# Opening of a two-block transformer kernel on one Trainium2 core: another order of loads and features, and products of zeros on TensorE

## The chip, the core and the metric

The kernel runs on one core of a Trainium2 chip, in one launch. The metric is the device time in microseconds (us) from the start of the program to its end. In the views of the profile PE is TensorE (PEld its weight loads), DVE is VectorE, ACT is ScalarE, POOL is GpSimd and SP is SyncE, which here only issues transfers (DMA).

## What is computed

Two transformer blocks over 256 tokens of width 1024, all in fp32. The first block has two layers with adaptive normalization and 256 context tokens beside the 256 tokens of x. The change touches only the first lines of layer 0:

```python
shift, scale, gate = adaln(c, ada_w[i], ada_b[i])          # silu(c) @ ada_w + ada_b
cshift, cscale, cgate = adaln(c_ctx, ada_w[i], ada_b[i])
h = rms_norm(x, pre_g[i]) * (1.0 + scale) + shift
hc = rms_norm(xc, pre_g[i]) * (1.0 + cscale) + cshift      # xc is the context
...
p = t @ w_in                                               # t is h, then hc; w_in is 1024 x 4096
q, k, v, z = jnp.split(p, ...)
```

After it come differential attention, a projection, a second layer with grouped attention, and a second block with sparse attention, retention and a gated feed-forward network. None of that is changed.

## The kernel before

**Products.** A product of features and weights in fp32 is made from three products in the rounded format fp32r: each operand is split into a rounded part (`hi`) and its rest (`lo`), and TensorE adds hi·hi, hi·lo and lo·hi in one PSUM bank (lines 746, 747, 748, in this order: `x_hi`·`w_hi`, `x_hi`·`w_lo`, `x_lo`·`w_hi`). Each moves 512 columns. A unit `gemm_unit(stage, c, t, ks)` does this for token tile t (0 and 1 are x, 2 and 3 the context), weight chunk c (512 columns) and the feature blocks `ks` of 128; `FIRST` is blocks 0 to 3, `SECOND` blocks 4 to 7. The projection of the first layer is the stage `in0`, with 8 chunks.

**Modulation.** `ada_half("ada0", c, h)` multiplies the silu of c and c_ctx (`cstat`) by half h of chunk c of `ada_w` (L768, fp32, 4 calls that appear in the trace as 8 records). Chunk 0 is the shift and chunk 2 the scale of feature blocks 0 to 3, chunks 1 and 3 those of blocks 4 to 7; `ADA0_ORDER` is 0, 2, 1, 3. ScalarE copies the rows out (`move`, L1297), `mod_columns` turns them into columns on TensorE (L782), and VectorE adds bias and gain (`mod_sums`, L1900 and L1905).

**Features.** ScalarE sums the squares of each token tile (`norm0_square`, L1254), GpSimd takes the power -1/2, VectorE scales the tile (`norm_in`, L1808, into `zbuf`, here called `xn`), and TensorE transposes it by blocks (`norm0_part`, L865, for blocks 0 to 3; `norm`, L813, for the others). Then `norm_modulated` on ScalarE and `norm_lo_modulated` on VectorE make, from the bank of each block, the modulated features of x (ScalarE, L1268) and of the context (VectorE, L1816) in `sc`, their rounded part `act_hi` (ScalarE, L1274) and the rest `act_lo` (VectorE, L1820), always 512 tokens at a time. TensorE waits for `act_ready` of block k before the first product with it.

**Loads.** SyncE issues the large loads from one queue, in the order of its program: c, c_ctx, the identity, then halves of 1 MB (1024 KB) each. ScalarE's queue loads x (1 MB) and small vectors; GpSimd's the rotary tables and other parameters. `modulation(c)` loads the two halves of chunk c of `ada_w` into four large buffers that are free at this time (`act_hi_as_f`, `kT`, `act_lo_as_f`, `vbuf` for chunks 0, 1, 2, 3). `stream(n)` loads half n of all later weights into one of six buffers (`raw`); from n = 6 on it waits until TensorE has emptied the buffer. A half is split by ScalarE (L1234) and VectorE (L1768) into `w_hi` (a ring of 3) and `w_lo`.

**Order.** Each engine has its own program, written out by hand; nothing is scheduled by a planner. On TensorE the opening is: the transposed silu; both halves of chunk 0 (`ada0(0)`); the transposed parameter vectors (L873); the columns of chunk 0; the transposes of x and then of the context; chunk 2 and its columns; chunk 1; and then the first units of `in0` with blocks 0 to 3, between which lie the transposes of blocks 4 to 7, the columns of chunk 1, and chunk 3 with its columns:

```python
ada0(2)
mod_columns(0, 2)
ada0(1)
gemm_unit("in0", 0, 0, ks=FIRST)
norm("norm0", range(4, 6))
mod_columns(0, 1)
gemm_unit("in0", 0, 1, ks=FIRST)
ada0(3)
gemm_unit("in0", 0, 2, ks=FIRST)
mod_columns(0, 3)
gemm_unit("in0", 0, 3, ks=FIRST)
norm("norm0", range(6, KT))
```

Then the same four units go through blocks 4 to 7, and `in0` goes on chunk by chunk.

## Time and profile before

| | us |
|---|---|
| median of 3 runs | 856.02 |
| lowest and highest | 856.01, 857.07 |
| the profiled execution | 854.07 |
| its span | 852.1 |
| PE busy in the span | 804.9 |
| DVE, ACT busy | 495.9, 395.1 |

The span is the time from the first to the last instruction of the profiled execution; 1.97 us of that execution lie outside it. All rows are from this execution. A row of the timeline gives the start, the duration, the engine, the line, the operation, and the count of instructions that it merges; in brackets stands how long the engine was idle before it, and what ended that. The end of a matmul is modelled and overlaps the next one, so two neighbouring rows are compared by their starts.

### The profile page before, as it was taken

How to read it: one execution, taken by the hardware profiler on the slowest of the kernel's cores; microseconds unless marked ns; L12 is line 12 of the kernel's file. 1: busy time of each engine (PE TensorE's matmuls, PEld its weight loads, DVE VectorE, ACT ScalarE, POOL GpSimd, SP SyncE). 2: the span in 40 equal slices, each digit the busy share in tenths (PEclk: the TensorE clock that was granted, in tenths of full speed). 3: DMA queues.
4: the chain of work that ended last, by engine and by line, in shares of the span. 5: the costliest groups of instructions: out<-in, count | busy, mean ns of one | idle time of the engine just before them, and what ended most of it. 6: DMA issues, size and time to landing. Idle time of an engine off the chain costs nothing. (4 is left out here: it accounts for less than half of the span.)

```text
span 852.1 us, 10720 instructions
## 1 busy us (share of the span) xinstructions
PE 804.9 (94%) x4000; PEld 621.2 (73%) x4000; DVE 495.9 (58%) x849; ACT 395.1 (46%) x718; POOL 39.9 (5%) x55
## 2 busy tenths in 40 slices
PE   4999999999998998999999999998989999999997
PEld 2577788776665677777766787776768888888886
DVE  3373433225557665779655666598786655545553
ACT  4342232326766672575655454544244443344431
POOL 1020000000001000011000001100010000000000
PEclk9999999999999999999999999899989999999999
DMA  9963554325000043239223034863114466646521
GB/s 344 386 207 117 198 197 178 107 111 198 2 1 0 1 150 123 100 101 346 93 78 99 1 128 172 295 231 100 38 49 142 162 221 204 198 149 210 186 98 50
DMA packets 70438, 122.92 MB, mean 144 GB/s; under 512 B 2618, under 2 KB 28556, under 8 KB 70260
## 3 DMA queue, kind: packets, MB, share of 16 engines
q1 hardware_dynamic: 69344, 119.85, 40.7%
q0 software_dynamic: 512, 1.18, 0.5%
q10 hardware_dynamic: 532, 1.21, 0.4%
q8 instruction: 32, 0.52, 0.3%
q14 instruction: 18, 0.15, 0.1%
HBM read 121.17 MB, written 1.06 MB: 143 GB/s over the span
## 5 line engine op out<-in xcount | busy, mean ns | idle before, releaser
L746 PE MATMUL psum<-w_hi,act_hi 128*128 128x512 f32 (+1 forms) x720 | 293.5, 408 | 2.1 <-DVE act_lo L1820 0.8
L747 PE MATMUL psum<-w_lo,act_hi 128*128 128x512 f32 (+1 forms) x752 | 293.5, 390 | 0.0
L748 PE MATMUL psum<-w_hi,act_lo 128*128 128x512 f32 (+1 forms) x720 | 281.0, 390 | 0.0
L1768 DVE TENSOR_TENSOR w_lo<-raw,w_hi 128x2048 fp32r<-128x2048 f32 (+1 forms) x79 | 178.7, 2266 | 147.3 <-ACT w_hi L1234 147.1
L1234 ACT ACTIVATE w_hi<-raw 128x2048 fp32r<-128x2048 f32 (+1 forms) x79 | 149.6, 1895 | 121.0 <-PE psum L748 46.3
L746 PEld LDWEIGHTS psum<-w_hi,act_hi 128*128 128x128 f32 x720 | 136.3, 189 | 56.8 <-issue 26.5
L747 PEld LDWEIGHTS psum<-w_lo,act_hi 128*128 128x128 f32 x752 | 142.5, 190 | 26.3 <-issue 1.2
L748 PEld LDWEIGHTS psum<-w_hi,act_lo 128*128 128x128 f32 x720 | 136.1, 189 | 29.3
L1736 POOL TENSOR_TENSOR rstd<-ms,half_neg 128x1 f32<-128x1 f32 (+3 forms) x38 | 33.5, 883 | 593.5 <-DVE ms L1791 593.5
L1368 ACT ACTIVATE sc<-psum,nmax 128x512 f32<-128x512 f32 (+1 forms) x64 | 36.7, 581 | 30.5 <-DVE nmax L1959 30.5
L1959 DVE TENSOR_REDUCE nmax<-psum 128x2 f32<-128x1024 f32 (+1 forms) x32 | 30.5, 956 | 33.1 <-PE psum L897 33.0
L846 PE MATMUL psum<-ident,sc 128*128 128x128 f32 x192 | 31.9, 282 | 18.2 <-DVE sc L1974 10.1
L846 PEld LDWEIGHTS psum<-ident,sc 128*128 128x128 f32 x192 | 21.6, 142 | 23.8 <-DVE sc L1974 13.7
L1297 ACT ACTIVATE sc<-psum 128x512 f32<-128x512 f32 (+1 forms) x60 | 32.3, 538 | 8.9 <-PE psum L846 8.0
L1297 ACT ACTIVATE qT<-psum 128x512 f32<-128x512 f32 (+1 forms) x24 | 13.2, 569 | 49.7 <-PE psum L840 32.9
L1198 PE MATMUL psum<-w_hi,act_hi 128*128 128x512 f32 x88 | 34.3, 390 | 0.8 <-DVE act_lo L2513 0.8
L1200 PE MATMUL psum<-w_hi,act_lo 128*128 128x512 f32 x88 | 34.3, 389 | 0.0
L1199 PE MATMUL psum<-w_lo,act_hi 128*128 128x512 f32 x88 | 34.2, 389 | 0.0
L1692 ACT ACTIVATE sc<-psum 128x256 f32<-128x256 f32 x22 | 8.4, 383 | 47.2 <-PE psum L748 47.2
L897 PE MATMUL psum<-kT,qT 64*128 64x512 f32 (+1 forms) x128 | 29.0, 533 | 0.0
L923 PEld LDWEIGHTS psum<-vbuf,sc 128*128 128x128 f32 x192 | 26.1, 191 | 3.6 <-ACT sc L1297 0.8
L923 PE MATMUL psum<-vbuf,sc 128*128 128x128 f32 x192 | 26.8, 276 | 0.0
(241 smaller groups left out, 882.3 us busy)
## 6 DMA issues: line engine op xcount, KB each, us to landing
raw<-in_a_w_in SPq DMA_DIRECT2D x16, 1024.0 KB, 9.6
raw<-in_ada_w SPq DMA_DIRECT2D x16, 1024.0 KB, 5.3
raw<-in_w_out SPq DMA_DIRECT2D x12, 1024.0 KB, 5.1
raw<-in_w_gate SPq DMA_DIRECT2D x22, 512.0 KB, 4.2
raw<-in_w_up SPq DMA_DIRECT2D x22, 512.0 KB, 5.3
raw<-in_w_down SPq DMA_DIRECT2D x11, 1024.0 KB, 5.0
raw<-in_b_w_in SPq DMA_DIRECT2D x10, 1024.0 KB, 8.0
raw<-in_w_in SPq DMA_DIRECT2D x10, 1024.0 KB, 10.0
```

The costliest lines, as they stand in the source:

```text
L746: pe.matmul(oh, x_hi, hi, start=(k == 0), stop=False)
L747: pe.matmul(o[:, 0:n], x_hi, lo, start=False, stop=False)
L748: mm = pe.matmul(oh, x_lo, hi, start=False, stop=(k == KT - 1))
L846: mm = pe.transpose(o[:, tile_cols(i)], src[:, tile_cols(i)], ident[:])
L923: mm = pe.matmul(o[:, 0:P], probs[:, tile_cols(i)], vbuf[:, NT - blocks + i, tile_cols(h)], start=(i == 0), stop=(i == blocks - 1))
L1198: pe.matmul(o, x_hi, hi, start=(j == 0 and i == 0), stop=False)
L1199: pe.matmul(o, x_hi, lo, start=False, stop=False)
L1200: mm = pe.matmul(o, x_lo, hi, start=False, stop=last)
L1234: ins = act.activation(hi, weights, ACTF.Copy)
L1297: seq.freed(act.activation(dst, src, ACTF.Copy, scale=scale).then_inc(bank_free(name), 1), name)
L1368: seq.freed(act.activation(sc[:, 2 * (p % 2) + s, 0:n], psum[:, b, 0:n], ACTF.Exp, bias=nmax[:, p % 2, s:s + 1], accum_out=rsum[:, p % 2, ...
L1768: ins = dve.tensor_tensor(rest, weights, hi.bitcast(F32), ALU.subtract)
```

## The change

It touches only the opening, up to the first units of `in0`.

- SyncE: half 0 of the streamed weights and both halves of chunk 2 (the scale) are loaded ahead of the two context tiles, not behind them.
- TensorE: the transposes of the context move from before chunk 2 to behind the first unit and chunk 1; chunk 1 moves from ahead of the first unit to behind it; the columns of chunk 1 come between the second and the third unit, and blocks 4 and 5 are transposed behind chunk 3. The transposes of x come ahead of the columns of chunk 0.
- TensorE: a new function `stay_awake(b, n)` issues n products of a 128x128 by a 128x512 block of zeros (fp32r) into bank b, whose contents nothing reads. There are 58 of them in seven places (16, 6, 9, 9, 7, 3, 8), all ahead of the first unit. VectorE fills their operand, a part of the last slot of the `w_hi` ring, at the very start (one copy of 128x640).
- ScalarE and VectorE: for blocks 0 to 3, the features are made first for x alone and later for the context alone, 256 tokens at a time. `first_hi` on ScalarE writes `act_hi` straight from PSUM, and for the even blocks also the modulated values; `first_lo` on VectorE makes the modulated values of the odd blocks, and `act_lo` for all. So x costs ScalarE six instructions and VectorE six. The squares of the context move behind the features of x on ScalarE, and its normalization behind them on VectorE. TensorE waits for the new semaphore `first_lo_ready` at the units of tile 0 and tile 2 only.

```diff
@@ sync
             modulation(ADA0_ORDER[0])
+            stream(0)
+            modulation(ADA0_ORDER[1])
             for t in range(XT):
                 load(xs[:, XT + t, :], a["ctx"][0, t * P:(t + 1) * P, :], s_ctxin)
-            stream(0)
-            modulation(ADA0_ORDER[1])
             modulation(ADA0_ORDER[2])
@@ tensor
+            def stay_awake(b, n):
+                for _ in range(n):
+                    pe.matmul(psum[:, b, :], idle_r[:, 0:P], idle_r[:, P:P + COLS], start=True, stop=True)
+
+            pe.wait_ge(s_idle, 1)
+            stay_awake(1, 16)
...
+            stay_awake(1, 6)
...
-            ada0(0)
+            ada_half("ada0", 0, 0)
+            stay_awake(1, 9)
+            ada_half("ada0", 0, 1)
...
+            norm0_part(FIRST, range(XT))
             mod_columns(0, 0)
-            norm0_part(FIRST, range(XT))
+            stay_awake(1, 9)
+            ada_half("ada0", 2, 0)
+            stay_awake(0, 7)
+            ada_half("ada0", 2, 1)
+            stay_awake(0, 3)
+            mod_columns(0, 2)
+            stay_awake(0, 8)
+            gemm_unit("in0", 0, 0, ks=FIRST)
+            ada0(1)
             norm0_part(FIRST, range(XT, NT))
-            ada0(2)
-            mod_columns(0, 2)
-            ada0(1)
-            gemm_unit("in0", 0, 0, ks=FIRST)
+            gemm_unit("in0", 0, 1, ks=FIRST)
+            mod_columns(0, 1)
+            gemm_unit("in0", 0, 2, ks=FIRST)
+            ada0(3)
             norm("norm0", range(4, 6))
-            mod_columns(0, 1)
-            gemm_unit("in0", 0, 1, ks=FIRST)
-            ada0(3)
-            gemm_unit("in0", 0, 2, ks=FIRST)
             mod_columns(0, 3)
@@ scalar
+            def first_hi(s, k):
+                name = ("norm0", k)
+                if s:
+                    act.wait_ge(*finished(name))
+                else:
+                    act.wait_ge(s_xturned, k + 1)
+                r = slice(XT * P * s, XT * P * (s + 1))
+                ps = psum[:, place[name][0], r]
+                scale, bias = mod[:, 0, 0, k, s:s + 1], mod[:, 0, 1, k, s:s + 1]
+                seq.note(act.activation(act_hi[:, k, r], ps, ACTF.Identity, scale=scale, bias=bias).then_inc(s_hi0, 1), s_hi0)
+                if k % 2:
+                    return
+                ins = act.activation(sc[:, 4 + k, r], ps, ACTF.Identity, scale=scale, bias=bias)
...
@@ vector
+            def first_lo(s, k):
...
+                if k % 2:
+                    dve.wait_ge(s_hi0, HALF_KT * s + k + 1)
+                    ins = dve.tensor_scalar(sc[:, 4 + k, r], psum[:, place[name][0], r], mod[:, 0, 0, k, s:s + 1],
+                                            mod[:, 0, 1, k, s:s + 1], ALU.mult, ALU.add)
...
+                seq.note(dve.tensor_tensor(act_lo[:, k, r], sc[:, 4 + k, r], act_hi[:, k, r].bitcast(F32),
+                                            ALU.subtract).then_inc(s_lo0, 1), s_lo0)
+
             mod_sums(0, 0)
-            norm_in("norm0", range(XT, NT))
             split_through(0)
             mod_sums(0, 2)
             dve.wait_ge(*seq.last)
-            for k in range(0, HALF_KT, 2):
-                norm_lo_modulated("norm0", 0, k, k + 2)
+            for k in FIRST:
+                first_lo(0, k)
+            norm_in("norm0", range(XT, NT))
+            for k in FIRST:
+                first_lo(1, k)
             split_through(1)
```

The next four listings show what stands in a row on an engine. First TensorE before, from its start to the first unit (L853 transposed silu, L768 modulation, L873 parameter vectors, L782 columns, L865 transposes, L746 to L748 the products of the unit):

```order
L853 MATMUL psum<-ident,vecs 128x16
L768 MATMUL psum<-act_hi_as_f,cstat 32x512 x8
L873 MATMUL psum<-ident,vecs 128x82
L782 MATMUL psum<-sel,qT 128x2 x4
L865 MATMUL psum<-ident,zbuf 128x128 x16
L768 MATMUL psum<-act_lo_as_f,cstat 32x512 x8
L782 MATMUL psum<-sel,qT 128x2 x4
L768 MATMUL psum<-kT,cstat 32x512 x8
L746 MATMUL psum<-w_hi,act_hi 128x512
```

TensorE after, at the same place (L863 is `stay_awake`, L777 the modulation, L892, L791 and L883 the vectors, columns and transposes), from the second half of chunk 0 on:

```order
L777 MATMUL psum<-act_hi_as_f,cstat 32x512 x4
L892 MATMUL psum<-ident,vecs 128x82
L883 MATMUL psum<-ident,zbuf 128x128 x8
L791 MATMUL psum<-sel,qT 128x2 x4
L863 MATMUL psum<-w_hi 128x512 x9
L777 MATMUL psum<-act_lo_as_f,cstat 32x512 x4
L863 MATMUL psum<-w_hi 128x512 x7
L777 MATMUL psum<-act_lo_as_f,cstat 32x512 x4
L863 MATMUL psum<-w_hi 128x512 x3
L791 MATMUL psum<-sel,qT 128x2 x4
L863 MATMUL psum<-w_hi 128x512 x8
L755 MATMUL psum<-w_hi,act_hi 128x512
```

Chunk 1 (`kT`) and eight of the sixteen transposes no longer stand ahead of the first unit; they follow behind its twelve products. ScalarE before, from the copy of chunk 0's rows to the first features (L1297 copy of rows, L1254 squares of the context, L1234 split of a weight half, L1268 and L1274 features):

```order
L1297 ACTIVATE qT<-psum 128x512 [waits bank0_full]
L1254 ACTIVATE sc,ss<-xs 128x1024 [waits bank0_free,ctx_in]
L1254 ACTIVATE sc,ss<-xs 128x1024 [waits square_sum_ready]
L1234 ACTIVATE w_hi<-raw 128x2048 [waits raw_landed0]
L1297 ACTIVATE qT<-psum 128x512 [waits bank1_full]
L1268 ACTIVATE sc<-psum,mod 128x256 [waits bank2_full,mod_rows_ready]
L1268 ACTIVATE sc<-psum,mod 128x256 [waits bank3_full]
```

ScalarE after, at the same place (L1310 and L1313 are `first_hi`, L1278 the squares):

```order
L1340 ACTIVATE qT<-psum 128x512 [waits bank0_full]
L1258 ACTIVATE w_hi<-raw 128x2048 [waits raw_landed0]
L1340 ACTIVATE qT<-psum 128x512 [waits bank1_full]
L1310 ACTIVATE act_hi<-psum,mod 128x256 [waits x_turned,mod_rows_ready]
L1313 ACTIVATE sc<-psum,mod 128x256
L1310 ACTIVATE act_hi<-psum,mod 128x256 [waits x_turned] x2
L1313 ACTIVATE sc<-psum,mod 128x256
L1310 ACTIVATE act_hi<-psum,mod 128x256 [waits x_turned]
L1278 ACTIVATE sc,ss<-xs 128x1024 [waits first_hi_ready,ctx_in]
L1278 ACTIVATE sc,ss<-xs 128x1024 [waits square_sum_ready]
L1340 ACTIVATE qT<-psum 128x512 [waits bank6_full]
```

The squares of the context now wait behind the six instructions that make the features of x.

## Rows read from the trace of the kernel before

**Rows 1.** The page: busy time of TensorE, and the transfers over 40 slices.
```profile
PE 804.9 (94%) x4000; PEld 621.2 (73%) x4000; DVE 495.9 (58%) x849; ACT 395.1 (46%) x718; POOL 39.9 (5%) x55
...
DMA  9963554325000043239223034863114466646521
```

**Rows 2.** Three stretches of TensorE: us, busy (records), granted clock, DMA share, GB/s.
```profile
28.00:29.00 1.00, 0.78 (x4) 0.54 1.04 385
60.00:80.00 20.00, 20.00 (x110) 1.00 0.47 159
540.00:560.00 20.00, 19.46 (x80) 0.83 1.02 357
```

**Rows 3.** Timeline of SyncE's queue: start and duration of the issue.
```profile
2.96 1.18 SPq L562 DMA_DIRECT2D xs<-in_ctx  x2
```

**Rows 4.** The loads of chunk 3 (tile vbuf): issue, first and last start, time to landing.
```profile
L580 SPq DMA_DIRECT2D vbuf<-in_ada_w x2: 2584/2584/2585, 19.2 to 21.8; - x2
...
DMA to landing us min/median/max: 14.6/15.2/15.8
```

**Rows 5.** Timeline of TensorE and its weight loads up to the first unit.
```profile
9.12 1.93 PE L768 MATMUL psum<-act_hi_as_f,cstat 128*32 128x512 f32 x8 [1.84 <-DMA act_hi_as_f<-in_ada_w]
...
12.32 1.93 PE L768 MATMUL psum<-act_hi_as_f,cstat 128*32 128x512 f32 x8 [1.27 <-DMA act_hi_as_f<-in_ada_w]
...
15.06 1.84 PE L782 MATMUL psum<-sel,qT 128*128 128x2 f32 x8 [0.48 <-ACT qT L1297]
...
21.36 3.55 PE L768 MATMUL psum<-act_lo_as_f,cstat 128*32 128x512 f32 x16
22.80 0.47 PEld L768 LDWEIGHTS psum<-act_lo_as_f,cstat 128*32 128x32 f32 x8 [1.24 <-DMA act_lo_as_f<-in_ada_w]
...
25.63 1.05 PE L782 MATMUL psum<-sel,qT 128*128 128x2 f32 x8 [0.73 <-ACT qT L1297]
...
26.61 1.06 PE L768 MATMUL psum<-kT,cstat 128*32 128x512 f32 x8
...
28.22 1.94 PE L768 MATMUL psum<-kT,cstat 128*32 128x512 f32 x8 [0.55 <-DMA kT<-in_ada_w]
```

**Rows 6.** Timeline of TensorE from the first unit to block 6.
```profile
30.09 0.79 PE L746 MATMUL psum<-w_hi,act_hi 128*128 128x512 f32 x1
...
30.68 0.63 PE L747 MATMUL psum<-w_lo,act_hi 128*128 128x512 f32 x1
...
31.11 0.58 PE L748 MATMUL psum<-w_hi,act_lo 128*128 128x512 f32 x1
...
33.72 1.03 PE L813 MATMUL psum<-ident,zbuf 128*128 128x128 f32 x8
...
38.33 1.92 PE L768 MATMUL psum<-vbuf,cstat 128*32 128x512 f32 x16
...
40.18 0.50 PE L746 MATMUL psum<-w_hi,act_hi 128*128 128x512 f32 x1
...
43.08 0.95 PE L782 MATMUL psum<-sel,qT 128*128 128x2 f32 x8
...
46.76 1.03 PE L813 MATMUL psum<-ident,zbuf 128*128 128x128 f32 x8
...
49.98 0.50 PE L746 MATMUL psum<-w_hi,act_hi 128*128 128x512 f32 x1 [0.81 <-DVE act_lo L1820]
```

**Rows 7.** Timeline of ScalarE and VectorE around the context's squares and the features.
```profile
15.01 1.06 ACT L1254 ACTIVATE sc<-xs 128x1024 f32<-128x1024 f32 x1
...
17.83 1.58 DVE L1808 TENSOR_SCALAR zbuf<-xs,rstd 128x1024 f32<-128x1024 f32 x2 [0.31 <-POOL rstd L1736]
...
24.98 0.60 ACT L1297 ACTIVATE qT<-psum 128x512 f32<-128x512 f32 x1 [5.71 <-PE psum L768]
...
27.12 1.02 ACT L1268 ACTIVATE sc<-psum,mod 128x256 f32<-128x256 f32 x2 [1.54 <-DVE mod L1905]
...
55.37 0.42 DVE L1860 TENSOR_TENSOR sc<-sc 128x256 f32<-128x256 f32 x1
```

More of the change, by code:

```diff
@@ L334, in block_kernel @@
         y_tok = vbuf
+        idle_r = w_hi[:, RING - 1, 0:P + COLS]
         q_flat = qT[:].rearrange("p h n -> p (h n)")
@@ L402, in block_kernel @@
         s_hsq = sem("head_square_sum_ready")
+        s_idle, s_xturned = sem("idle_operands_ready"), sem("x_turned")
+        s_hi0, s_f0, s_lo0 = sem("first_hi_ready"), sem("first_x_modulated"), sem("first_lo_ready")
         s_res, s_yret = sem("residual_ready"), sem("retention_head_done")
@@ L679, in block_kernel @@
         h_base, n = {}, 0
-        for stage, count in (("norm0", 8), ("turn_o0", 8), ("norm1", 8), ("norm1c", 8), ("turn_o1", 4), ("norm2", 4),
+        for stage, count in (("norm0", 4), ("turn_o0", 8), ("norm1", 8), ("norm1c", 8), ("turn_o1", 4), ("norm2", 4),
                              ("turn_o2", 4), ("norm3", 4), ("hidden", 2 * FFN_STEPS)):
@@ L725, in act_ready @@
                     return
-                if src in act_base:
+                if src == "norm0" and k < HALF_KT:
+                    if t in (0, XT):
+                        pe.wait_ge(s_lo0, HALF_KT * (t // XT) + k + 1)
+                elif src in act_base:
                     if t == 0:
@@ L865, in norm0_part @@
                         mm = pe.transpose(o[:, tile_cols(t)], xn[:, t, k * P:(k + 1) * P], ident[:])
-                    if tiles[0]:
-                        mm.then_inc(bank_full(name), 1)
-            ada0(0)
+                    mm.then_inc(bank_full(name) if tiles[0] else s_xturned, 1)
+            ada_half("ada0", 0, 0)
+            stay_awake(1, 9)
+            ada_half("ada0", 0, 1)
             pe.wait_ge(s_vec, 16 * N_VEC)
@@ L1323, in _ @@
             move(mod_rows(0, 0), ("ada0", 0, 0))
+            split_through(0)
+            move(mod_rows(0, 2), ("ada0", 2, 0))
+            act.wait_ge(s_mod, 1)
+            for k in FIRST:
+                first_hi(0, k)
             act.wait_ge(s_ctxin, 16 * XT)
@@ L1326, in _ @@
             norm0_square(3)
-            split_through(0)
-            move(mod_rows(0, 2), ("ada0", 2, 0))
-            for k in range(0, HALF_KT, 2):
-                norm_modulated("norm0", 0, k, k + 2)
+            move(mod_rows(0, 1), ("ada0", 1, 0))
+            for k in FIRST:
+                first_hi(1, k)
             split_through(1)
-            move(mod_rows(0, 1), ("ada0", 1, 0))
             move(mod_rows(0, 3), ("ada0", 3, 0))
@@ L1868, in rot_free @@
                     dve.wait_ge(*finished(rot_units[n - 3]))
+            dve.wait_ge(s_half, 1)
+            seq.note(dve.tensor_copy(idle_r, zero[:].broadcast_to((P, P + COLS))).then_inc(s_idle, 1), s_idle)
             dve.wait_ge(s_silu, 1)
@@ L1912, in _ @@
             dve.wait_ge(*seq.last)
-            for k in range(0, HALF_KT, 2):
-                norm_lo_modulated("norm0", 0, k, k + 2)
+            for k in FIRST:
+                first_lo(0, k)
+            norm_in("norm0", range(XT, NT))
+            for k in FIRST:
+                first_lo(1, k)
             split_through(1)
```

21 lines of the change are left out of this document (18 added, 3 removed).

## The prediction

> **What bounds the kernel now.** The page comes first: TensorE is busy for 804.9 of 852.1 us, and the transfers fill their engines only in the first two slices [rows 1]. From about 50 us on TensorE works without a gap (20.00 us busy of 20) [rows 2], so whatever the opening saves reaches the end, if TensorE only starts that stretch earlier. The place to read is therefore the timeline up to block 6 of the second pass, at 49.98 us, where TensorE waits for the last time in the opening (0.81 us, for `act_lo`) [rows 6].
>
> Before the first unit TensorE waits for bytes: half 0 of chunk 0 at 9.12, half 1 at 12.32, half 1 of chunk 2 (the scale) at 22.80, half 1 of chunk 1 at 28.22 [rows 5]. Between the last two lie two halves of 1 MB, so a half takes (28.22 - 22.80) / 2 = 2.71 us; the queue is full, and the order of the loads is the time of their landing. The other thing to see is the clock. Eight records of L768 take 1.93 us at 9.12 and 12.32, and 1.06 at 26.61; the columns take 1.84 at 15.06, 1.05 at 25.63 [rows 5]. These are the two levels, 1.2 and 2.4 GHz. In 28 to 29 the granted clock is 0.54 [rows 2], after gaps of 0.73 and 0.55 us around columns and a modulation half, and the first products of the unit still run at half rate (30.68 to 31.11 is 0.43 us for one; 12 between 40.18 and 43.08 are 0.24 each) [rows 5, 6].
>
> **The change, part by part.** I follow the path after the change and compare at one point: the transposes of blocks 6 and 7, at 46.76 before [rows 6].
>
> 1. *Loads.* Two context tiles, 1 MB in all, issued at 2.96 before [rows 3], go behind the scale. Its half 1 lands one half earlier, at 22.80 - 2.71 = 20.1, half 0 at 17.4. The context lands at 22.8 instead. Chunk 1 (28.2) and chunk 3 (21.8 + 15.8 = 37.6) [rows 4] keep their places in the queue.
>
> 2. *From the scale to the features of x.* Before, from the landing at 22.80 to the end of the products at 24.91 (21.36 + 3.55), then the copy of the rows at 24.98 and the first feature on ScalarE at 27.12: 2.21 us from the end of the products [rows 5, 7]. After, the half costs 1.06 at full clock, so the features start at 20.1 + 1.06 + 2.21 = 23.4. The three products of zeros between (0.7 us) lie under the 0.60 us copy and its waits.
>
> 3. *Features of x alone.* ScalarE needs two instructions (0.51 each, 27.12) before VectorE can make the first `act_lo` of 256 columns (0.42, the nearest row is 55.37) [rows 7]: the first unit starts at 23.4 + 1.02 + 0.42 + 0.1 = 24.9, and was at 30.09 before. ScalarE needs 6 x 0.51 = 3.1 for all four blocks (to 26.5), VectorE another 0.1 + 0.5 + 0.42, and the last three products 0.7: the unit ends near 28.2. Chunk 1 has landed (28.2), its products take 1.85 (38.33 to 40.18) [rows 6]: TensorE is free at 30.1.
>
> 4. *The context behind it.* Its squares now wait in ScalarE's queue behind the six instructions, until 26.5. Before, from the first square (15.01) to the end of both scaled tiles (17.83 + 1.58) are 4.4 us [rows 7]; the second power need not wait for the first now, which I put at 0.2. The transposes of the context start at 26.5 + 4.2 = 30.7. This, not TensorE at 30.1, is the later arm. The late landing (22.8) costs nothing as long as ScalarE comes to it at 26.5; if ScalarE came before 22.8, it would show.
>
> 5. *The rest of the opening.* From 33.72 to 46.76 TensorE did, in another order, exactly what now follows the context's transposes: three units, chunk 3, two columns, eight transposes, 13.04 us with no gap [rows 6]. Added are the context's eight transposes, 0.87 (33.72 to the columns at 34.59, counted from the 1.03 less overlap). So the compare point is at 30.7 + 13.9 = 44.6, against 46.76: 2.2 us. The columns of chunk 3 then come 2.2 earlier too, and the chain to block 6 (46.76 to 49.98) is unchanged. Chunk 3 is reached at 30.7 + 0.9 + 2.9 + 0.9 + 2.9 = 38.3, its second half at 39.2, with 37.6 landed: covered by 1.6 us. If this cover went, each us of lateness would be on the path.
>
> 6. *Products of zeros.* 58 in all. VectorE's copy of 640 columns should be over near 2 us (0.42 for 256 [rows 7], plus the start). The first 16 cost 16 x 0.43 = 6.9 at half clock, 16 x 0.24 = 3.8 at full. Half 0 of chunk 0 lands at 9.1, and ahead of it stand the transposed silu and 6 more (1.4). If the clock rises only with the last of the 16, TensorE comes to it at 10.3, 1.2 late; if it rises halfway, in time. From there the row is tight: from 12.32, 0.93 + 0.2 + 0.87 + 0.85 + 9 x 0.24 + 0.93 + 7 x 0.24 gives 19.9 for the second half of the scale, which lands at 20.1. So up to 1 us of lateness is handed on nearly whole. Between 0 and 1 I take 0.1 as the likeliest, near the lower end, because nothing interrupts these 16, and rows 5 show the rise from 1.93 to 1.06 behind the steady work that starts at 21.36.
>
> The Trainium skill (TensorE: Matmul & The Clock Gate, Part 1) says that the throttled state is the default and that activity releases it, and that the number of slow matmuls at a start differs from run to run of one kernel. Rows 5 show both levels but only one start, so no row here bears out the variation. It speaks for both bounds of step 6, and gives no other value.
>
> The same skill (DMA: Bandwidth & Descriptors, section HWDGE ordering) warns that completion is not first in, first out for an issuing engine. Here halves land in order, 2.71 us apart, so the trace does not show it; were it to hold for the context and the scale, the 2.71 of step 1 would be less, and that is rival B.
>
> 7. *Cheap edits.* The wait of `norm_modulated` for `first_lo_ready` is met long before. VectorE's second split (2.3 us of L1768) comes between the context's `act_lo` (35.5) and the columns of chunk 3 (41.4). GpSimd's rotary load is issued after the later powers, some 2 us later than before, needed after 50. Columns of chunk 1 (34.5) find their rows copied at 31. Nothing is late by these.
>
> Sum: 2.2 - 0.1 = 2.1 us off the span of 852.1, so 850.0; with the 1.97 outside, 852.0 for a profiled execution. The median of the runs is 1.95 above the profiled 854.07; I take the gain off the median: 856.02 - 2.1 = **853.9**.
>
> **Rivals.**
> A, the forecast: gain 1.7 to 2.8, between the context's arm at 4.4 with 0.1 more of zeros and the arm of TensorE at 30.1 ruling. 853.2 to 854.3.
> B, gain shrinks: the 16 zeros run at half clock to the end (0.9 late), or the clock falls once more in the stretch of transposes and columns near 14 to 16 us, as it fell at 28 before. There, 9 zeros, one half and part of 7 would cost 0.2 more each and 0.9 for the half, 1.2 in all after what waits absorb. Gain 1.0 to 1.7, time 854.3 to 855.2, say 854.9. For it: the fall in rows 2 came after such a mix. Against: the mix in 33.72 to 35.4 kept the clock.
> C, more: no lateness, TensorE rules at 30.1 and the last wait of 0.81 shrinks too: gain 3.3, 852.7. Against: `act_lo` for block 6 comes from transposes that stand at the same distance.
> D, slower: the clock stays at half until the scale. Then 47 zeros ahead of its second half cost 0.43 each. From 2.0: 6.9, silu 0.3, 2.6, 1.93, 3.9, 1.93, 0.4, 2.0, 1.84, 3.9, 1.93, 3.0, 1.93 gives 34.6 where step 2 has 21.2, so 13.4 later, 11.3 slower net: 867.3. It decides at about 11 zeros and one half slow on the path behind 12.3 us (2.1 / 0.2). Before, with gaps of 1.84 and 1.27, the clock was still at half at 15, so it is not excluded; continuous zeros make it improbable.
> E, the gain is made and lost: chunk 3 or later weights land too late, since TensorE comes 2 us earlier to a full queue. Cover is 1.6 at chunk 3, and the next halves are used after 55. Time 855.5 to 856.
>
> **How the numbers follow.** A 0.52, B 0.26, C 0.07, D with its milder forms 0.08, E 0.07. The clock in later stages (0.83 in 540 to 560 [rows 2]) and the spread of the runs (1.06) add some 0.5 us to each. A measurement of this kernel tells 0.2%, 1.7 us, from no change. A beyond 1.7 less its noise, C, and a bit of B make faster 0.55; most of B, some of A and E make same 0.37; slower 0.08. The range for 8 in 10 takes A, B, C and most of E: 852.2 to 856.0.
>
> **What would show it.** Right: zeros from about 2 us; the products at 12.3 at 1.06 per eight records; the scale's second half at 20.1 and context landed at 22.8; first unit at 24.9; context's transposes at 30.7 waiting for `zbuf`; blocks 6 and 7 transposed at 44.6; block 6 at 47.8. Wrong: rows of L777 at 1.93 behind zeros (B, D); a wait for `vbuf` (E); a first unit that starts at 24.9 while block 6 is still at 49 (a new wait behind the context). The forecast fails first if step 4 is mis-sized, since it alone sets the later arm.

## The result and the profile after

The changed kernel takes 859.31 us (median of 9 runs, 857.0 to 860.29), the kernel before on the same chip 856.02 (9 runs, 855.02 to 860.17): ratio 1.0031, 95% interval 1.0018 to 1.0045. The prediction was 853.9, faster, in a range of 852.2 to 856.0. It is slower by 0.3%, and outside the range. The profiled execution takes 859.58 us, its span is 857.6.

The busy time and the transfers of the changed kernel, against [rows 1]: TensorE is busy for 12.8 us more (817.7) in 58 records more (4058), and its first slice is full now. From the page, with the queues of the transfers: packets, MB, share.

```profile
PE 817.7 (95%) x4058; PEld 632.0 (74%) x4058; DVE 497.9 (58%) x854; ACT 396.1 (46%) x722; POOL 40.2 (5%) x55
...
PE   9999999999998998999999999999979999999997
...
q1 hardware_dynamic: 69344, 119.85, 40.7%
q0 software_dynamic: 512, 1.18, 0.5%
q10 hardware_dynamic: 532, 1.21, 0.4%
q8 instruction: 33, 0.54, 0.2%
```

The opening on TensorE, against [rows 5, 6]: start, duration, line, operation, count, and in brackets the wait before and who ended it. L863 are the products of zeros, L777 the modulation, L791 the columns, L883 and L822 the transposes.

```profile
1.46 6.80 PE L863 MATMUL psum<-w_hi 128*128 128x512 f32 x16 [1.46 <-DVE w_hi L1918]
...
8.36 1.67 PE L863 MATMUL psum<-w_hi 128*128 128x512 f32 x6
9.96 1.06 PE L777 MATMUL psum<-act_hi_as_f,cstat 128*32 128x512 f32 x8
...
13.23 1.06 PE L777 MATMUL psum<-act_hi_as_f,cstat 128*32 128x512 f32 x8
...
21.10 1.06 PE L777 MATMUL psum<-act_lo_as_f,cstat 128*32 128x512 f32 x8
...
26.08 0.47 PE L755 MATMUL psum<-w_hi,act_hi 128*128 128x512 f32 x1 [0.17 <-DVE act_lo L1972]
...
31.75 1.09 PE L883 MATMUL psum<-ident,zbuf 128*128 128x128 f32 x8 [0.58 <-DVE zbuf L1854]
...
45.65 1.03 PE L822 MATMUL psum<-ident,zbuf 128*128 128x128 f32 x8
...
48.87 0.50 PE L755 MATMUL psum<-w_hi,act_hi 128*128 128x512 f32 x1 [0.81 <-DVE act_lo L1866]
```

The first 16 products of zeros cost 0.425 us each on the mean, which is the lower level of the clock; from then on all is at the upper one up to 262 us (1.06 for eight records of the modulation, where [rows 5] have 1.93). The first unit starts 4.0 us earlier than before, but block 6 only 1.11 (48.87 against 49.98). So the opening gives half of the 2.1 that I expected.

The rest is lost behind the opening. TensorE waits at two places where the first trace of before shows no wait (its timeline):

```profile
102.24 0.50 PE L755 MATMUL psum<-w_hi,act_hi 128*128 128x512 f32 x1 [1.16 <-DVE sc L1900]
...
181.58 0.50 PE L755 MATMUL psum<-w_hi,act_hi 128*128 128x512 f32 x1 [0.85 <-ACT vbuf L1340]
```

I matched the products of the two traces one by one, counted back from the last, and took the difference of their starts. It is -1.11 us at 100, +0.31 at 150, +1.48 at 200 (each wait costs a little more than its bracket), +1.38 at 255, and +5.42 at the end. The last 4.0 are mostly stretches at the lower clock, which other executions of before have too; they are taken up below, behind the waits.

### The profile page after: what moved, and what is told of

It is laid out like the page before. It is cut to its first block and busy times, and to the rows that moved or that the text cites. A ratio compares the mean times of both kernels' runs of the same rounds, so it can differ in the third digit from the quotient of the medians.

```text
span 857.6 us, 10845 instructions
## 1 busy us (share of the span) xinstructions
PE 817.7 (95%) x4058; PEld 632.0 (74%) x4058; DVE 497.9 (58%) x854; ACT 396.1 (46%) x722; POOL 40.2 (5%) x55
## 3 DMA queue, kind: packets, MB, share of 16 engines
HBM read 121.17 MB, written 1.06 MB: 143 GB/s over the span
## 5 line engine op out<-in xcount | busy, mean ns | idle before, releaser
L1814 DVE TENSOR_TENSOR w_lo<-raw,w_hi 128x2048 fp32r<-128x2048 f32 (+1 forms) x79 | 178.9, 2266 | 150.6 <-ACT w_hi L1258 150.4
L1782 POOL TENSOR_TENSOR rstd<-ms,half_neg 128x1 f32<-128x1 f32 (+3 forms) x38 | 33.6, 885 | 613.2 <-DVE ms L1837 613.1
```

The source lines that it names most:

```text
L1814: ins = dve.tensor_tensor(rest, weights, hi.bitcast(F32), ALU.subtract)
```

## The experiments

**Theory 1: code.** Behind the waits stands a half of 1 MB that lands late. A half is written in 16 shares, and it has landed with the last. Besides the data, the trace's DMA records show transfers of 16 KB of the kind `instruction` (q8 in the page): 32 in the kernel before, with its 8000 records of TensorE (a product and its weight load are two), and 33 in the changed one, with 8116. So one comes for about 250 of these records, and I take them for the fetch of TensorE's code.

Before they start at 33.6, 54.7, 77.3, 102.9, 127.9, 150.8, 176.5, after at 21.7, 49.8, 68.4, 93.3, 115.8, 142.5, 167.8: the 58 products are 116 instructions more, and the transfers come 5 to 12 us earlier, most of them some 9. Now for the bursts of loads of weights. Before, the transfers behind 75 us start between the bursts (86.4 to 98.3, 112.1 to 124.0, 138.7 to 150.6, 164.8 to 176.6, by the packets of q1) or at a burst's end. After, the four at 93.3, 115.8, 142.5 and 167.8 all start inside a burst (85.3 to 98.6, 112.3 to 125.3, 139.0 to 152.1, 165.1 to 178.2).

In each of these four bursts one share of every half that lands after it is 1.4 to 1.7 us behind the median of the 16; before, the last share is 0.2 to 0.4 behind. TensorE waits behind two of the four: there one half landed at 94.73 by the median and 96.43 by the last share (before 95.83 and 96.14), another at 174.49 and 176.02 (before 174.21 and 174.40). ScalarE's split waits for the last share. Its timeline in the changed kernel, and in the kernel before under it:

```profile
84.31 1.92 ACT L1258 ACTIVATE w_hi<-raw 128x2048 fp32r<-128x2048 f32 x1 [1.72 <-PE psum L757]
...
96.46 1.92 ACT L1258 ACTIVATE w_hi<-raw 128x2048 fp32r<-128x2048 f32 x1 [8.45 <-DMA raw<-in_a_w_in]
```

```profile
85.42 1.92 ACT L1234 ACTIVATE w_hi<-raw 128x2048 fp32r<-128x2048 f32 x1 [1.72 <-PE psum L748]
...
96.17 1.92 ACT L1234 ACTIVATE w_hi<-raw 128x2048 fp32r<-128x2048 f32 x1 [7.05 <-DMA raw<-in_a_w_in]
```

All of it starts 1.11 earlier (84.31), and still the second split is 0.29 later. VectorE's split (98.41) and its rotation (L1898 to L1900, ready at 102.2) follow, and TensorE, 1.11 early, waits for them. **Theory 2:** the waits come from the change of order itself, as TensorE arrives early at a queue that is full anyway (rival E); then they are there whenever TensorE is early, whatever the number of its instructions. **Theory 3:** they belong to that execution.

*The zeros left out of the changed kernel* (nothing that is used is left out, here and in all that follow):

```diff
-                for _ in range(n):
+                for _ in range(0 * n):
```

> The kernel after, without any of the 58 products of zeros; load order, feature order and the position of the units stay. Theory 1: TensorE has 116 instructions less, the code loads fall outside the bursts as before, no wait at 102 and 182. The opening is then at half clock: the scale's second half lands near 20.2, its products take 1.9, the columns 1.8, so the first unit starts near 27 and block 6 near 49.5 to 50.5, against 49.98 before. Time within 1 us of before, 855.5 to 857. Rival 2: a start that is no earlier than before makes no waits either, so this run alone does not part 1 from 2; it gives the share of the loads and features without the zeros. Rival 3: 857 or more, by stretches at half clock after 260 us.

857.72 us, ratio 1.0017 (1.0002 to 1.0032), 0.7 above what I expected at most. There is no wait at 102 or 182, but TensorE comes 0.8 late here, so this run does not part theory 1 from theory 2. What it shows is the clock, which stays low up to the first unit (TensorE's timeline):

```profile
9.39 1.94 PE L777 MATMUL psum<-act_hi_as_f,cstat 128*32 128x512 f32 x8 [1.98 <-DMA act_hi_as_f<-in_ada_w]
...
20.52 1.94 PE L777 MATMUL psum<-act_lo_as_f,cstat 128*32 128x512 f32 x8 [0.74 <-DMA act_lo_as_f<-in_ada_w]
...
27.18 0.77 PE L755 MATMUL psum<-w_hi,act_hi 128*128 128x512 f32 x1 [2.14 <-DVE act_lo L1972]
...
50.80 0.50 PE L755 MATMUL psum<-w_hi,act_hi 128*128 128x512 f32 x1 [0.81 <-DVE act_lo L1866]
```

Block 6 is at 50.80, 1.93 later than with zeros. The zeros do what they are for; the new order without them loses 0.8 in this trace.

*The kernel before with 58 products of two columns at its start,* the same 116 instructions with nearly no work in them:

```diff
+            pe.wait_ge(s_idle, 1)
+            for _ in range(58):
+                pe.matmul(psum[:, 1, 0:2], idle_r[:, 0:P], idle_r[:, P:P + 2], start=True, stop=True)
             pe.wait_ge(s_cin, 16 * N_CIN)
```

> The kernel before, with 58 products of zeros of 2 columns each on TensorE at its very start, where it waits until 7 us anyway (and VectorE's copy of the operand). Nothing else is changed: loads, order and features are those of before. It adds the same 116 TensorE instructions as the change (58 weight loads, 58 products), but next to no time. Theory 1 (code loads): the trace after shows a 16 KB transfer of kind instruction at 93.3 us, inside the burst of weight loads, and one of the 16 shares of the half that lands at 94.9 comes at 96.43 instead, so that TensorE waits 1.16 us at 102.2. Added instructions shift these transfers by 8 to 10 us. So this kernel should show such a wait near 103 and 182 us, and be 1.5 to 2.5 us slower than before (857.5 to 858.5). Rival 2 (the earlier start): the waits come because TensorE reaches these places 1.1 us sooner than the loads; then this kernel has none of them and stays within 0.5 us of before. Rival 3 (clock): the loss is made by stretches at half clock after 260 us alone; then it is also as before.

865.57 us, ratio 1.0114 (1.0093 to 1.0136), where I expected 858.5 at most. The waits are there, as theory 1 has it. But the products are not free. TensorE's timeline:

```profile
1.47 12.53 PE L854 MATMUL psum<-w_hi 128*128 128x2 f32 x58 [1.47 <-DVE w_hi L1880]
...
107.49 0.50 PE L748 MATMUL psum<-w_hi,act_hi 128*128 128x512 f32 x1 [0.96 <-DVE sc L1862]
...
186.55 0.50 PE L748 MATMUL psum<-w_hi,act_hi 128*128 128x512 f32 x1 [0.58 <-ACT vbuf L1305]
```

0.216 us each for two columns, where 512 columns cost 0.425 at the same clock. Each product still has its weight load (0.29 to 0.33 us in this trace, and they overlap), which is the likely reason; no run tests it. The products moved the opening by 4.35 us as well, so this run alone does not part the number of instructions from the time. In its trace TensorE is 4.35 late at 60, 6.42 at 255 and 9.75 at the end.

*The zeros cut to 256 columns,* twice as many, with 12 small ones: 128 products, 256 instructions, the work of the changed kernel otherwise.

```diff
-                for _ in range(n):
-                    pe.matmul(psum[:, b, :], idle_r[:, 0:P], idle_r[:, P:P + COLS], start=True, stop=True)
+                for _ in range(2 * n):
+                    pe.matmul(psum[:, b, 0:COLS // 2], idle_r[:, 0:P], idle_r[:, P:P + COLS // 2], start=True, stop=True)
             stay_awake(1, 16)
+            for _ in range(12):
+                pe.matmul(psum[:, 1, 0:2], idle_r[:, 0:P], idle_r[:, P:P + 2], start=True, stop=True)
```

> The kernel after, with each product of zeros cut in two of 256 columns, plus 12 of 2 columns behind the first 16: 128 products, 256 TensorE instructions more than before instead of 116, for about the same columns. Code is loaded in pieces of 16 KB, about 256 TensorE instructions apart in the trace, so the loads fall back to where they lie in the kernel before. Theory 1: opening as after (block 6 near 48.9), no wait at 102 and 182, time 1 us below before, 854.5 to 855.5. Rival 2 (earlier start): the waits at 102 and 182 stay, 857.5 to 859.5. Rival 3 (clock): waits gone or not, stretches at half clock after 260 us keep it at 858 to 859.

857.63 us, ratio 1.0016 (1.0003 to 1.0029). The instruction transfers are at 102.2, 127.2, 150.2 and 175.7, as before, no share between 75 and 190 us is more than 0.6 behind its median, and the waits at 102 and 182 are gone, though TensorE comes 0.66 us early. TensorE is nearly as early (0.72) in a second trace of the changed kernel (a1, below), which has both waits; the first is this row of its timeline:

```profile
102.25 0.51 PE L755 MATMUL psum<-w_hi,act_hi 128*128 128x512 f32 x1 [0.79 <-DVE sc L1900]
```

So neither the new order nor an early TensorE makes the waits, and these two runs settle theory 1 against theory 2. The time is a miss all the same: I expected 854.5 to 855.5, and this kernel is slower than before with no wait left. Its trace is 0.71 early at 255 us and 2.60 late at the end.

*The same with 106 products of 256 columns* (212 instructions; 22, 12, 16, 18, 14, 6, 18 at the seven places), so that the transfers fall between the bursts:

```diff
-            stay_awake(1, 16)
+            stay_awake(1, 22)
```

> The kernel after with zeros of 256 columns in place of 512, in counts 22, 12, 16, 18, 14, 6, 18 instead of 16, 6, 9, 9, 7, 3, 8: 106 products, 212 TensorE instructions more than before. The first block is a third shorter, so that TensorE reaches the transposed silu at 7.2 instead of 8.2. Theory 1: code loads fall some 3 us later than in e3, between the bursts; no waits at 102 and 180; the two late starts of the zeros (0.6 us at the first half of chunk 0, 0.5 at the second half of the scale) go, so block 6 near 48.3 instead of 48.9. Time 0.5 to 1.5 us under before (855 to 856). Rival 2: the waits are back, since TensorE is earlier still: 858 to 859. Rival 3: 857 to 858 as e3.

855.89 us, ratio 0.9985 (0.9973 to 0.9998). The transfers are at 79.5, 104.9, 128.2, 154.3 and 180.5, between the bursts, and no wait stands at 102 or 182. The one at 18.0 falls into the opening. There the last share of the scale's second half landed 1.57 behind the median (0.48 in the half ahead of it), and TensorE waited for it:

```profile
21.45 1.06 PE L777 MATMUL psum<-act_lo_as_f,cstat 128*32 128x512 f32 x8 [0.84 <-DMA act_lo_as_f<-in_ada_w]
...
49.24 0.50 PE L755 MATMUL psum<-w_hi,act_hi 128*128 128x512 f32 x1 [0.81 <-DVE act_lo L1866]
```

*The new order of loads alone, in the kernel before:*

```diff
-            for t in range(XT):
-                load(xs[:, XT + t, :], a["ctx"][0, t * P:(t + 1) * P, :], s_ctxin)
             stream(0)
             modulation(ADA0_ORDER[1])
+            for t in range(XT):
+                load(xs[:, XT + t, :], a["ctx"][0, t * P:(t + 1) * P, :], s_ctxin)
```

> The kernel before, with the new order of loads alone: half 0 of the streamed weights and the scale ahead of the context. The scale's second half lands near 20.5 and the context near 23.2. But ScalarE's queue still has the context's squares ahead of the split and of the copy of the scale's rows, so these wait for 23.2 + 2.3 + 1.9: rows copied near 27.4 in place of 24.98, first unit near 32.5, and 1.5 to 2.5 us slower than before. It would show that the load order gains nothing without the features of x alone. Rival: if time stays within 0.5 us of before, the first unit has slack in before that step 5 of the prediction did not see.

864.52 us, ratio 1.0090 (1.0066 to 1.0113). ScalarE's timeline, and TensorE's:

```profile
23.45 1.06 ACT L1254 ACTIVATE sc<-xs 128x1024 f32<-128x1024 f32 x1 [8.07 <-DMA xs<-in_ctx]
```

```profile
27.88 1.97 PE L865 MATMUL psum<-ident,zbuf 128*128 128x128 f32 x8 [8.71 <-DVE zbuf L1808]
...
37.52 0.47 PE L746 MATMUL psum<-w_hi,act_hi 128*128 128x512 f32 x1 [1.34 <-DVE act_lo L1820]
```

My expectation (1.5 to 2.5 slower) was right in sign and far too small in size: not only ScalarE has the context ahead of the scale, TensorE's row has its transposes there too. The new loads need the x-only features on all engines.

*Later split.* ScalarE and VectorE work through their programs in order, so a split that waits for a late share holds up all that stands behind it. In this run the first half of the chunk after the next is split one unit later, ahead of the second unit of the next chunk and no longer at the end of the present one, while all 58 zeros stay (on both engines):

```diff
                 for t in tiles:
+                    if stage == "in0" and c and t == 1:
+                        split_through(g0 + 2)
                     if t == tiles[-1] and not before_norm:
...
-                run_chunk("in0", c, unit0)
+                run_chunk("in0", c, unit0, ahead=3)
```

> The kernel after, zeros and all (116 instructions more, code loads inside the bursts), with one change on ScalarE and VectorE in the first projection: the split of the first half of chunk c+2 is done ahead of unit (c+1, 1) and no longer at the end of chunk c. So the late share of a weight half has nothing behind it that TensorE needs soon. Theory 1: code loads are where they are in after, one share of the half is still 1 to 1.7 us late, but the waits at 102 and 182 are gone: 1.5 to 2.4 us faster than after, 856.5 to 858 beside a before of 856 to 857.2. If the waits had another cause (rival 2, the earlier start as such, or TensorE's own row of work), they stay and the time is that of after.

858.17 us, ratio 1.0014 (0.9997 to 1.0031), 0.2 above the expected range. The late shares are there (95.53 against a median of 94.1), the waits are not: TensorE is 1.59 us ahead of the first trace of before at 60 us and 1.62 ahead at 255. So late shares harm only where no slack takes them up. But the same trace is 5.24 late at the end: it loses 6.86 past 255, the most of all, with no wait at 102 or 182. The same edit in the kernel before changes nothing:

> The kernel before, with only the later split of e8. Its profiles b1 and b2 show a wait of 0.46 and 0.54 us at 102.8, its first profile none. Theory 1: 0 to 0.6 us faster than before. So e9 against this one is the worth of the opening alone, about 1.5 us. If the later split gained 2 us here too, it would be a gain of its own and not a cure of what the change brought.

856.42 us, ratio 1.0004 (0.9992 to 1.0015). And the later split in the changed kernel again, with 11 and 8 zeros in place of 16 and 9, to be in time for the first halves:

```diff
-            stay_awake(1, 16)
+            stay_awake(1, 11)
...
-            stay_awake(1, 9)
+            stay_awake(1, 8)
```

> As e8, and with 11 and 8 zeros of full width in place of the first 16 and 9 (52 in all, 104 instructions). The prediction's step 6 had TensorE late by up to 1 us behind the first 16; the trace of after shows chunk 0's first half begun at 9.96 against a landing of 9.36 and the scale's second half at 21.10 against 20.58. Expected: 9.4 and 20.6, no code load in the first 20.5 us (in e5 it fell at 17.96 and made the scale land at 21.4), block 6 near 48.4, no wait at 102 and 182. 1.0 to 2.2 us under before. If the clock stays at half for lack of zeros, the opening loses 1 to 2 us instead and it equals before.

858.35 us, ratio 1.0029 (1.0013 to 1.0044): a miss. Its first half is met in time (9.82, a wait of 0.40 for the bytes), but block 6 is at 48.83, since the second half of the scale landed at 20.91 and TensorE started it at 21.05. The trace is 1.14 ahead at 255, and the time is still above before.

**What lies past 255 us.** These last runs say that something more than the waits costs time. So I took more traces of both kernels as they are, and of the variant with fewer halves, with and without the later split. The kernels named "again", "third" and so on have no edit (b2, b5 and a3 repeat b1, b4 and a2, with the same expectations); the one with fewer halves and the later split has the two edits shown above.

> The kernel before once more, unchanged, for a second profile of it. The first one (854.07) is 2.2 us under the mean of its 18 timed runs, and has full clock at 262, 333 and 526 us, where the profiles of the kernel after, of e1, e2 and e3 each have a stretch of 3.4 us at half clock. Theory 1a: these stretches come in most executions of any of the kernels, and are no effect of the change; then this profile has two or three of them, and its span is 853.5 to 855.5. Rival 3 (the change brings them): none at 262, 333, 526, span 852 to 853.

> The changed kernel once more, nothing edited. Theory 1 (the 116 added instructions of TensorE move the 16 KB instruction transfers into the bursts of weight loads near 93 and 168 us, so that a share of a half lands late): the transfers are again near 21.7, 49.7, 68.4, 93.3 and 167.8 us, TensorE waits again near 102 and 182 us (0.5 to 1.2 each), and the opening ends again 1.1 us earlier than before (block 6 at 48.9). The time is 1 to 3 us over before. Rival (chance: the two waits belonged to that one execution): no wait at 102 or 182, and the time differs from before by less than 1 us.

> The products of zeros as 106 of 256 columns (212 instructions, as in the kernel with fewer halves), and the split of the first half of each later chunk one unit later on ScalarE and VectorE. Theory 1: the instruction transfers stay near 79 and 105 us and no share is late, so the later split has nothing to mend: the time is that of the kernel with fewer halves within 0.5 us, that is 0.8 to 1.8 us under before. Rival (the split one unit later costs something of its own, which the two kernels with it also paid): the time is 1 to 2 us above the kernel with fewer halves, so equal to before or over it.

> The kernel before, nothing edited, for one more profile. Read against its first profile, up to 255 us: 0 to 0.8 us late (a wait near 102). Past 255 theory 1 expects 0 to 5 us of lateness by stretches at the lower clock that fall otherwise in each execution. The rival expects 2.5 us or less here, clearly less than in the changed kernel.

> The changed kernel, nothing edited, for one more profile. Up to 255 us both expect 1.3 to 1.5 us late against the first profile of before. Past 255 theory 1 (the opening and the two waits are all that is the change's own) expects 0 to 5 us more, as in before. The rival (the change also makes the stretches at the lower clock past 255 us longer, 1.5 to 2 us on average) expects 4 to 6 us.

> The kernel before against itself: ratio 1.000, within 0.0013 of it if the comparisons are as sharp as their intervals say. Its trace past 255 us: 2.4 to 4.3 us late against its first profile, as in three of the four others.

> The changed kernel with its products of zeros as 106 of 256 columns (212 instructions of TensorE), once more. If its gain is real, 1.3 us under before again (0 to 2.5), no wait at 102 or 182 us, first trace of before less than 0.7 us at 255 us. If the first result was chance: equal to before or above it.

What came of them is best read as a table: how late TensorE is against the first trace of before, in us, with the products matched from the end, and beside it the time in us (the median, and the ratio with its interval where several runs were timed; a ratio is against the kernel before timed beside it, whose median ran from 856.0 to 857.2, so medians of different rows compare roughly).

```
                                  at 60   at 255   at end   past 255    time    ratio
before, first                      0.00     0.00     0.00      0.00    856.02
before, again (b1)                +0.04    +0.72    +4.44      3.72    858.59
before, again (b2)                +0.18    +0.75    +4.60      3.85    858.69
before, third (b4)                +1.70    +1.70    +5.96      4.26    860.18
before, fourth (b5)               -0.29    +0.02    +2.40      2.38    856.49
before, fifth (b6)                +0.24    +0.45    +1.38      0.93    856.36  0.9998 (0.9986-1.0010)
after, first                      -1.11    +1.38    +5.42      4.04    859.31  1.0031 (1.0018-1.0045)
after, again (a1)                 -0.72    +1.35    +7.00      5.65    860.25  1.0027 (1.0011-1.0043)
after, third (a2)                 -1.02    +1.28    +5.65      4.37    859.86
after, fourth (a3)                -0.99    +1.21    +6.03      4.82    860.11
fewer halves (e5)                 -0.72    -0.73    +1.75      2.48    855.89  0.9985 (0.9973-0.9998)
fewer halves, again (e5b)         -0.50    -0.34    +4.86      5.20    856.74  0.9997 (0.9985-1.0009)
fewer halves, later split (e10)   +0.44    +0.38    +3.86      3.48    856.41  0.9998 (0.9983-1.0014)
no zeros (e2)                     +0.80    +0.75    +2.80      2.05    857.72  1.0017 (1.0002-1.0032)
half width (e3)                   -0.66    -0.71    +2.60      3.31    857.63  1.0016 (1.0003-1.0029)
later split (e8)                  -1.59    -1.62    +5.24      6.86    858.17  1.0014 (0.9997-1.0031)
later split, fewer zeros (e9)     -1.14    -1.14    +3.09      4.23    858.35  1.0029 (1.0013-1.0044)
```

Theory 3 is out: all four traces of the changed kernel have both waits, 0.79 to 1.16 and 0.69 to 0.85 us. Before has a smaller wait near 102 in two of its six (0.46 and 0.54 us), where a share of the half was late too (the last at 96.96 and 97.09, 1.1 and 1.2 behind the median), and none near 182. In these two no transfer of 16 KB starts inside the burst. A small one of 8 KB (`instruction` too, on q14) does, at 87.7 and 87.6, and took 0.90 and 1.19 us, where the first trace has it at 87.5 with 0.31 and no late share. That fits theory 1, but nothing tests it. With these two exceptions the twenty traces of all kernels fall in two clean groups between 75 and 190 us: in all 28 bursts in which a transfer of 16 KB starts before the last 1 us, a share is 1.2 to 1.8 us behind, and in the 50 others none is more than 0.72 behind.

The means of four and of six give the account:

- the opening: -0.96 against +0.31, so 1.27 gained. In its third trace before is late by itself, as the clock is still low in the first unit: TensorE's timeline there has rows like this up to 33.8, where the first trace, at the lower level in 30.68 to 31.11 as well [rows 6], is at the upper one from 31.5 on.

```profile
33.82 0.63 PE L747 MATMUL psum<-w_lo,act_hi 128*128 128x512 f32 x1
```

- from 60 to 255, the waits: +2.27 against +0.30, so 1.97 lost.
- past 255: 4.72 against 2.52, so 2.2 lost.

Together 2.9 us, where the two comparisons of timed runs give 3.3 and 3.8 by the medians and 2.7 and 2.3 by the ratios. Past 255 the losses are steps of 1.2 to 1.7 us (2.6 once) at the same places in the work of either kernel, where the clock falls. The windows (us; busy us and records of PE, PEld, DVE, ACT and POOL; granted clock, DMA share, GB/s) at two of them, in the first trace of before, in its third, and in the first of after:

```profile
255.00:275.00 20.00, 16.69 (x91) 11.07 (x90) 13.65 (x23) 14.34 (x44) 3.31 (x2) 1.00 0.00 0
325.00:345.00 20.00, 17.85 (x83) 14.01 (x83) 8.96 (x17) 8.49 (x12) 0.20 (x1) 1.00 0.10 29
```

```profile
255.00:275.00 20.00, 16.96 (x82) 11.58 (x81) 13.82 (x25) 13.93 (x39) 3.31 (x2) 0.91 0.00 0
325.00:345.00 20.00, 17.85 (x77) 13.92 (x76) 9.20 (x23) 5.47 (x10) 1.64 (x1) 0.91 0.21 76
```

```profile
255.00:275.00 20.00, 16.96 (x82) 11.65 (x81) 13.89 (x24) 13.90 (x39) 3.31 (x2) 0.91 0.01 1
325.00:345.00 20.00, 17.85 (x76) 13.51 (x75) 8.92 (x22) 5.58 (x11) 1.64 (x1) 0.91 0.22 79
```

Just ahead of both places TensorE waits for VectorE, 2.5 and 2.15 us, in traces in which the clock then falls and in traces in which it does not. It falls at 262 in four of six traces of before and in four of four of after, at 334 in three of six and four of four. Of the 2.2 us some 0.35 are a wait that every kernel with the new opening shows and none with the old one, with or without zeros:

```profile
434.38 0.44 PE L849 MATMUL psum<-ident,sc 128*128 128x128 f32 x2 [0.36 <-DVE ss L2240]
```

The other 1.9 stay open. The ranges overlap (4.04 to 5.65 against 0 to 4.26), and a kernel with the new opening and no wait at 102 has 2.48 in one trace and 5.20 in the next. So it may be chance in ten traces, or an arrival that makes the falls likelier; what sets them I did not find. The traces of the variants lean to the second. All eleven with the new opening, with or without zeros and waits, lose 4.2 past 255 on the mean, and the clock falls at 262 in eleven and at 334 in ten; the nine with the old opening lose 2.7, and it falls in six and in five. So this loss does not need the waits at 102 and 182. By the same means the changed kernel without these two waits would still be 0.9 slower (1.27 gained, 2.2 lost).

The first result of the kernel with fewer halves did not come back in full (0.9985, then 0.9997), and before against itself gives 0.9998. With the later split it gives 0.9998 too. That is level with before, as its rival expectation has it, but not for the rival's reason: its opening is 0.44 late in the trace, as TensorE waited 1.31 for the first half and 1.22 for the scale's second half, whose last share landed 2.49 behind the median. None of the versions that I ran is surely faster than before.

## Why the prediction was wrong

Between the forecast (2.1 us off) and the means of the traces (2.9 on) lie 5.0 us: 0.8 in the opening, 2.0 in the waits, and 2.2 past 255, of which 1.9 stay open.

*Steps 1 and 2, the scale:* the second half landed at 20.58, not 20.1: 2.18 us earlier than before, not 2.71. The features started at 24.38, not 23.4. Of the 0.98, 0.48 is the landing, and 0.52 is TensorE, which came at 21.10 because the zeros before it (7, from 19.28) ran past the landing. The 2.21 us behind the products held (22.16 to 24.38). The landing was late by its last share: the median of the 16 is 19.91, but from the first half on one share was 0.68 behind the others. In the other three traces of the changed kernel that share was 1.35, 1.10 and 0.89 behind, and the scale landed at 21.34, 20.97 and 21.06. In the six of before it was 0.2 to 1.05 behind, 0.28 in the one that I predicted from. So the 20.1 came from a trace near the early end. No transfer of instructions starts in any trace between 0.3 and 16 us, where this lag begins, so what holds the share back is open.

*Step 3, the features of x:* right. The first unit came 1.70 us behind the first feature (26.08), as against 1.5.

*Step 4, the context's arm:* right, 7.37 us from the first feature to the transposes (31.75), against 7.3, and it was the later arm: TensorE waited 0.58 for `zbuf`.

*Step 5, the rest:* exact, 13.90 from there to the compare point (45.65), and 3.22 to block 6.

*Step 6, the zeros, is the step that failed,* twice. First in its lateness, 0.1 by the sum, 0.5 at the scale by the trace. All but the last two of the 16 ran at the lower clock, close to its upper bound and to rival B, and TensorE came to the first half 0.60 late. From there the row gave nothing back: from the first to the second half of the scale the products and seven zeros take 2.81 us (18.29 to 21.10, and 2.81 to 2.83 in the other three traces), where I had 0.93 + 7 x 0.24 = 2.6, and two landings are 2.7 apart. In the other three traces the lateness has another source. There the 16 took 6.21, 6.55 and 6.42 us, TensorE was in time and waited for the bytes of the first half (0.82, 0.17, 0.35), and it started the scale's second half at 21.49, 21.14 and 21.21, 0.15 to 0.17 behind its landing. There the late share of step 1 sets the time, and zeros that end sooner could not have gained more than these 0.2. The opening's gain of 1.11 lies in rival B (1.0 to 1.7), which I gave 0.26. For the clock I argued from a row that stands 21 us into the kernel ([rows 5], 21.36); the rows of the opening itself were at the lower level up to 15.06, and they were the nearer ones. The Trainium skill (TensorE: Matmul & The Clock Gate, Part 1) says that the number of slow matmuls at a start differs from run to run. The four traces of the changed kernel bear it out: 14, 11, 12 and 12 of the 16 came at the slow spacing of 0.43 us.

Second, the step counted the zeros only in time. As instructions they had a price too, which the sum put at nothing: 1.97 us by the means of four and six traces, through transfers which stand in the page of before as a line of 0.2% (q8). Rival E had the symptom, later weights that land late, but for another reason (TensorE comes early to a full queue), at another place (chunk 3) and its worst was a gain of nothing. The run with 256 instructions shows that the reason was not it.

*Step 7, cheap edits:* nothing seen up to 255. The wait at 434 was in no step, and neither was a loss past 255; these 2.2 us alone eat up the forecast gain. They go against the sentence ahead of the steps that whatever the opening saves reaches the end.

*The median:* taking the gain off the median of 856.02 was right; the first profile of before (854.07) is the best of its six spans (852.1 against 853.5 to 858.1). Against it the first profile after is 5.5 us longer; the mean of the four spans after is 2.9 longer than the mean of the six.

## What to carry to other kernels

Instructions added to TensorE, even with nothing in them, moved every later transfer of code against the transfers of data here. Where a load has no slack, look at its last share, not the median, and either choose their number so that the fetches fall between bursts or give the consumer slack. Work put into a wait for bytes must be over before the bytes come: count it at the lower clock. And take more than one trace of the kernel before: the one that I predicted from was 1.4 to 6.0 us shorter than the five others.

## What the hardware showed that I had not expected

- Transfers of 16 KB of the kind `instruction`, one for about 250 records of TensorE, each 0.9 to 1.5 us long. Between 75 and 190 us a share of a 1 MB half landed 1.2 to 1.8 us behind the median of the 16 in each of the 28 bursts of loads in which one started (seven traces, twenty in all looked at).
- In the first 16 us one share lags 0.2 to 1.4 us behind the others, from the first half on and in both kernels, with no such transfer near. It differs from execution to execution, and the later halves in the queue keep the lag.
- A product of 128x2 costs 0.216 us at the lower clock, half of one with 512 columns (0.425).
- The first 16 products of zeros took 6.21 to 6.80 us in the four traces of the changed kernel; behind them the upper clock held up to 255 us. Without them the modulation (1.94) and the start of the first unit (0.77 at 27.18) were at the lower one.
- The clock falls at the same two places of the work (262 and 334), each behind a wait of TensorE, in some executions and not in others.
